# Hybrid attention pairs of a transformer kernel: order of bank hand-backs, projection groups and waits changed

## The reference

```python
def _hybrid_mixer(u, positions, w_in, b_f, w_out):
    fq, fk, fv, ff, dq, dk, dv, iq, iw, ik = jnp.split(u @ w_in, offsets, axis=-1)
    log_f = jax.nn.log_sigmoid((ff + b_f).astype(jnp.float32))
    out_a = _fox_attention(fq..., fk..., fv..., log_f)       # 8 heads of 64, causal, with a forget gate
    dq = _rope(dq...); dk = _rope(dk...); iq = _rope(iq...); ik = _rope(ik...)
    out_b = _dsa_attention(dq, dk, dv..., iq, iw, ik)        # 8 heads of 64 over the 128 best keys a query
    return concatenate([out_a, out_b]) @ w_out
```

## Time and profile before

| | us |
|---|---|
| median of 3 runs | 3437.28 |
| lowest, highest | 3435.66, 3439.84 |
| the profiled execution, its own time | 3440.07 |
| its span in the trace | 3438.3 |

### The profile page before, as it was taken

The page is one execution under the profiler, slowest core; times in us unless marked ns, Lnnn a source line. Parts: engine busy times, 40 slices in busy tenths (PEclk is TensorE's granted clock), DMA queues, the critical chain, the costliest instruction groups (busy, mean ns, idle before and its releaser), DMA issues.

```text
span 3438.3 us, 40845 instructions
## 1 busy us (share of the span) xinstructions
PE 3390.9 (99%) x16326; PEld 2808.9 (82%) x16326; DVE 2206.8 (64%) x4409; ACT 607.3 (18%) x1298; POOL 36.9 (1%) x42
## 2 busy tenths in 40 slices
PE   9999999999999999999999999999999999999999
PEld 6888877768888888888578888877678856888888
DVE  7776859767767777565356544553355567687754
ACT  2000023231000010001331000023411243011100
POOL 0000000000000000000000000010000000000000
PEclk9999999999999999999999999999999999999999
DMA  6433512213434444332112222222222211222222
GB/s 262 156 132 139 185 65 99 82 40 129 151 128 156 149 159 159 110 114 91 45 50 86 86 86 87 85 88 82 63 81 86 75 68 62 86 86 86 86 80 80
DMA packets 63075, 355.72 MB, mean 103 GB/s; under 512 B 6260, under 2 KB 17140, under 8 KB 33140
## 3 DMA queue, kind: packets, MB, share of 16 engines
q1 hardware_dynamic: 62887, 353.12, 29.4%
HBM read 350.83 MB, written 9.34 MB: 105 GB/s over the span
## 4 chain that ended last, share of the span: by engine, by line
PE 88%; DVE 7%; issue 2%; DMA 1%; ACT 1%; SPq 0%; DVEq 0%; ACTq 0%
PE lin L431 34%; PE turn L431 30%; PE lin L538 4%; PE lin L370 4%; PE turn L370 3%; PE score L1731 2%; PE out L431 2%; PE out L1760 1%; PE lin L535 1%; DVE work L1059 1%; DMA normed_T<-in_ada 1%; PE turn L1745 1%; DVE work L3259 1%; PE score L708 1%; PE out L481 1%
## 5 line engine op out<-in xcount | busy, mean ns | idle before, releaser
L431 PE MATMUL lin<-normed_sums,weight_ring 128*128 128x256 f32 x2960 | 691.8, 379 | 0.2 <-DVE normed_sums L634 0.2
L431 PEld LDWEIGHTS lin<-normed_sums,weight_ring 128*128 128x128 f32 x2960 | 561.3, 190 | 76.3 <-DVE normed_sums L634 0.6
L431 PE MATMUL turn<-normed_sums,weight_ring 128*128 128x256 f32 x1928 | 454.7, 379 | 0.4 <-DVE small L3278 0.4
L431 PEld LDWEIGHTS turn<-normed_sums,weight_ring 128*128 128x128 f32 x1928 | 365.6, 190 | 50.5 <-DVE small L3278 0.8
L431 PE MATMUL turn<-normed_T,weight_ring 128*128 128x256 f32 x1704 | 389.0, 379 | 1.3 <-DVE work L3325 1.3
L431 PE MATMUL lin<-arena,weight_ring 128*128 128x256 f32 x1606 | 369.2, 379 | 1.8 <-DVE weight_ring L602 1.5
L431 PE MATMUL turn<-arena,weight_ring 128*128 128x256 f32 x1620 | 368.5, 380 | 1.7 <-DVE weight_ring L602 1.1
L431 PEld LDWEIGHTS turn<-normed_T,weight_ring 128*128 128x128 f32 x1704 | 323.3, 190 | 45.4 <-DVE work L3325 1.7
L431 PEld LDWEIGHTS turn<-arena,weight_ring 128*128 128x128 f32 x1620 | 306.8, 190 | 44.0 <-DVE weight_ring L602 1.9
L431 PEld LDWEIGHTS lin<-arena,weight_ring 128*128 128x128 f32 x1606 | 304.0, 190 | 44.7 <-DVE weight_ring L602 2.3
L431 PE MATMUL lin<-normed_T,weight_ring 128*128 128x256 f32 x1272 | 296.0, 379 | 0.0
(11 more groups left out here) (375 smaller groups left out, 3801.1 us busy)
## 6 DMA issues: line engine op xcount, KB each, us to landing
weight_ring<-in_up SPq DMA_DIRECT2D x110, 1024.0 KB, 4.8
arena<-in_ada SPq DMA_DIRECT2D x54, 768.0 KB, 4.4
weight_ring<-in_down SPq DMA_DIRECT2D x40, 1024.0 KB, 5.0
normed_T<-in_ada SPq DMA_DIRECT2D x36, 768.0 KB, 4.6
weight_ring<-in_down SPq DMA_DIRECT2D x20, 768.0 KB, 4.2
weight_ring<-in_dil_qk SPq DMA_DIRECT2D x9, 1024.0 KB, 4.9
weight_ring<-in_hyb_qk SPq DMA_DIRECT2D x8, 1024.0 KB, 4.8
weight_ring<-in_xbc SPq DMA_DIRECT2D x6, 1024.0 KB, 4.7
```

Of the source, the lines that this page charges most:

```text
L431: last = pe.matmul(o[:, at + n * H:at + (n + 1) * H], weight_block(slot, pairs, block, kp), op(kind, kp0 + kp), start=opens and g != "f" a ...
```

## The change

Four edits. (1) In the pairs (`bank_first=p >= 0`) VectorE does both combinations of c before the weight sums of stages 2 and 3. (2) Group b of the value slab 1 moves from pair 1 to pair 0. (3) Scores of pairs 0 to 3 wait for the count noted at their own slab's copies; those of the later pairs only for their rotations; the copies of a value slab are awaited in step 1 of the even pair that first uses it. (4) In pair 6 the fill has 32 units instead of 24: the two rotations stand in steps of their own, with gaps between and behind.

```diff
-        def product_step_dve(v, c, g, ahead=True):
+        def product_step_dve(v, c, g, ahead=True, bank_first=False):
...
             elif g == "c":
-                combine_c(v, c, lambda: sums(2))
+                if bank_first:
+                    combine_c(v, c)
+                    sums(2)
+                else:
+                    combine_c(v, c, lambda: sums(2))
                 sums(3)
...
-            0: QK[1] + VALUES[1][:1],
-            1: VALUES[1][1:] + QK[2] + QK[3][:1],
+            0: QK[1] + VALUES[1][:2],
+            1: VALUES[1][2:] + QK[2] + QK[3][:1],
...
-            6: QK[7][3:] + gap(4) + ROTS + gap(10),
+            6: QK[7][3:] + ROTS[:1] + gap(7) + ROTS[1:] + gap(15),
...
                 if name[-1] == "d" and last:
                     c.add("used", 2)
+                    c.n[f"copied_{name[0]}{name[1]}"] = c["used"]
...
-                    product_step_dve(e, c, name[-1])
+                    product_step_dve(e, c, name[-1], bank_first=p >= 0)
...
                 def start(p):
-                    e.wait_ge(products_used, c["used"] if p else c["first_qk"])
+                    if p < 4:
+                        e.wait_ge(products_used, c[f"copied_qk{p}"])
...
                 def fill(t):
-                    if t == 1:
-                        e.wait_ge(products_used, c["first_v"])
+                    p, at = divmod(t, STEPS)
+                    if at == 1 and p < 8 and p % 2 == 0:
+                        e.wait_ge(products_used, c[f"copied_v{p // 2}"])
```

More of the change, by code:

```diff
@@ L2155, in pe @@
                     fill_pe(e, c, -1, t)
-                c.n["first_qk"] = c["used"]
                 c.add("forget", 2)
@@ L2178, in pe @@
                     fill_pe(e, c, -1, t)
-                c.n["first_v"] = c["used"]
                 all_taken(e, c)
```

## The result

| | kernel before | changed kernel |
|---|---|---|
| median of 17 runs each, one chip | 3438.11 us | 3445.70 us |
| lowest, highest | 3435.60, 3443.31 | 3441.96, 3448.90 |
| the profiled execution, its own time | 3440.07 | 3441.96 |
| its span | 3438.3 | 3440.1 |

The ratio of the changed kernel to the kernel before is 1.0019, 95% interval 1.0012 to 1.0025: slower, by 4.1 to 8.6 us. That was outside the predicted range, 3432.5 to 3442.5.

A forecast was written before the change was run, and what follows sets the result against it. TensorE, busy 99% of the span, was taken as the bound, with 14.5 us of idle in the pairs to win. The terms, +2.3 - 0.7 = +1.6 us on the median 3437.28, gave 3438.9 us, range 3432.5 to 3442.5.

The forecast's parts named there:

- Banks first: In c groups of the pairs: dependent combinations 0.72 us apart, bank free 0.48 us sooner, VectorE 0.24 us more per group.
- The value group: Value group b moved to pair 0: a 2.7 us TensorE wait in pair 1, +3.0 us at the start of pair 3.
- Waits moved: Ahead of pair 4: 0.64 us copies' wait goes, norm wait grows 0.24 us; its first scores come +2.8 us.
- Pair 6: End of pair 6, ahead of pair 7's first scores: 0.38 to 0.75 us won, taken as 0.7.
- The clock: Rival: TensorE's clock falls in pair 1, 1.7 to 3.4 us on top, say 3441.5 us; chance 0.2.
- The sum: Whole kernel, with the wait and at full clock: +2.3 - 0.7 = +1.6 us, 3438.9 us; chance 0.38.
- VectorE keeps up: Rival: one VectorE idle in pair 0 doesn't come, pair 1's bank is free when wanted; -0.9 us, 3436.4 us; chance 0.25.
- The resolution: Whole kernel: 0.2%, 6.9 us, is about what a measurement tells from no change; same 0.91, faster 0.05, slower 0.04.
- the signs of being wrong: Pair 1 has no idle and ends before 577, or pair 6 is more than 1.5 us shorter.

The follow-up runs named there:

- no_move: The changed kernel with value group b back in pair 1, the other three edits kept: 3438.94 us, ratio 0.9999 to the kernel before.
- keep_busy: The changed kernel with five extra products into an unused bank just ahead of the wait in pair 1: 3443.31 us, ratio 1.0014.
- keep_both: The changed kernel with extra products into an unused bank, three in pair 0 and five in pair 1, ahead of the waits: 3443.53 us, ratio 1.0012.
- a_again: The changed kernel run again unaltered for a second profile: 3445.72 us, ratio 1.0017 to the kernel before.
- before_third: The kernel before with a third bank in the ring of the pairs and nothing else: 3440.81 us, ratio 1.0004.
- no_move_third: The changed kernel with the fills of pairs 0 and 1 as before and a third bank in the ring: 3439.74 us, ratio 1.0002.

## Why the prediction was wrong

By its own steps:

- **Banks first: right.** The combinations stand 0.72 us apart, c costs 0.24 us more (pair 0 of no_move is 25.93 - 25.68 = 0.25 us longer), the rotations wait 0.47 and 0.46 us where 0.94 stood, 0.45 forecast.
- **The value group: right in mechanism and size, at full clock.** Forecast: a transposition at 535.2 behind 1.6 us of idle, scores of pair 1 at 544.2, a new wait of 2.7 us up to 559.65, scores of pair 2 at 580.1. Measured: 535.14 and 1.52; 544.16; 2.51 us to 559.79; 582.13, which without the clock's 1.6 us is 580.5. At the first scores of pair 7 the order costs 2.55 us by keep_busy; the forecast's steps gave 2.3 - 0.4 = 1.9. The missing 0.6 us arise in pair 1 (64.56 us after the first scores, forecast 580.1 - 516.13 = 63.97).
- **Waits moved: right in the sum.** The copies' wait ahead of pair 4 is gone, but the norm wait ahead of it grew by 0.72 us, from 0.79 to 1.51, where 0.24 were forecast. From the first scores of pair 3 to those of pair 4 it is 0.2 us less than before, as forecast.
- **Pair 6: right where the clock allows.** Its scores come 0.3 us sooner (16.93 to 16.62), and pair 7 up to the output projection takes 14.42 and 14.43 us in the first and third changed profile, 14.81 before: 0.7 us in all. In the second, whose fall begins 2.3 us ahead of pair 7, both gains are gone (16.95 and 14.81). keep_both, whose fall begins just ahead of pair 7, takes 15.3 us for pair 7. So the 0.7 us come in some executions, and I had counted them in all.
- **The clock: the step that failed.** The sum was made at full clock; the fall in pair 1 stood beside it as a rival at 0.2, and a fall in pair 0 nowhere. The price of the first, 1.7 to 3.4 us, was about right (1.6), but it comes in three of three profiles. What I forecast for pair 0, 1.6 us of idle in the place of 0.40, came as 1.52, and behind it the clock fell in two of five profiles, at a price of 3.2 us (TensorE was busy 1.88 of 3.40 us ahead of it in a_again). I had measured both by the one fall of the trace before, behind 1.59 of 3.50 us busy, as if nothing milder could do it; no row said so.
- **What the clock does not explain.** The forecast was 1.6 us of loss. The medians give 7.6, the ratio 4.1 to 8.6. The means of the profiles up to the output projection give 232.9 - 228.0 = 4.9 us (2 of before, 3 of after), 2.7 of it the two falls and the rest order. And keep_both, with neither fall in its profiles, still has a median of 3443.53 us, 1 us above the range. So the order was undersized as well, by 0.6 us at pair 7 and some 1 us at the output projection, and the 1.7 us between these 4.9 and the ratio's middle of 6.6 lie inside its interval and stay without a place. Even the rival with the fall in pair 1, 3441.5 us, was 4 us too low.
- **The rival "VectorE keeps up" is out.** Both idles of VectorE in pair 0 came, 0.99 and 1.06 us for the 1.2 and 0.95 forecast, and the wait in pair 1 with them.
- **The resolution.** 6.9 us was given as what a measurement tells from no change. With 17 runs each, the interval is 2.2 us to either side. None of the signs of being wrong that the prediction listed has come, since none of them was about the clock.

The page TensorE: Matmul & The Clock Gate of the Trainium skill (The HAM clock gate) has the fall follow an idle of the engine. These traces agree: TensorE was busy 1.21 and 1.88 of 3.40 us ahead of the two falls, and with the wait in pair 1 filled by products no fall came there in four of four profiles. The page VectorE: DVE Perf Modes of the Trainium skill (The DRAIN you can't avoid) has a semaphore in a chain cost nothing extra. That was not borne out here: the combination that waits for the one before it started 0.72 us behind it; in the kernel before, with an independent weight sum between the two, the starts were 0.60 us apart.

## What to carry to other kernels

Two engines that exchange work step by step lose where a step's last product is the one the other engine needs first: compare, step by step, what the fill closes with what the other engine has to do, and move the work that is free to lie anywhere (here the searches) before moving the fill. A wait of TensorE in dense work can have a second price, the clock behind it, 1.6 and 3.2 us here. Put it into the sum with the share of executions in which you expect it, and not beside the sum as a rival: here it came behind four of four waits of 2.3 to 2.5 us in pair 1, two of five of 1.52 us in pair 0, and none of those of 1.51 us in pair 3. A single profile can be the quickest of 17 executions: landmarks inside the stage compare kernels to 0.03 us where medians can't.

## What the hardware showed that I had not expected

The same wait of 1.52 us in the same kernel was followed by 6.8 us at half clock in one execution and by none in two. What the half clock costs depends on the work under it. 3.4 us of it in pair 7 cost nothing (14.43 us against 14.42 without a fall), 6.8 us at the end of pair 6 and in pair 7, where TensorE waits anyway, cost 0.7 us, 3.4 us in pair 1 cost 1.6 and 6.8 us in pair 0, which is dense, 3.2. The share of time at a low clock doesn't give its cost. In before_third removing waits for banks lowered the clock (0.9945 for 0.9964 in the mean), and its profile has one gathered wait with a fall behind it; in no_move_third a like wait had none.
